# One block up to the output projection, with the sample attention merged into the gates stage

## The chip, the cores and the metric

The kernel runs on one core of a Trainium2 chip. A core has five engines with a queue of instructions each: TensorE (PE), VectorE (DVE), ScalarE (ACT), GpSimd (POOL) and SyncE (SP), which here only issues transfers, and 16 DMA engines. The engines run side by side and meet at semaphores. The metric is the device time of one execution in microseconds (us).

## The reference, cut to what matters

One layer of a hybrid decoder for 1024 prompt tokens and 64 sample tokens (8 sequences of 8), 1088 in all, width 1024, in float32:

```python
p = split(x @ w_in)                        # GLA, FoX, conv and three gates
o_gla  = gla(p) ; o_conv = B * conv3(C * h)
o_fox  = softmax(q k^T / 8 + decay, causal) v            # prompt: 8 heads, 1024 keys
o_fox_s = the same for the sample; per sequence 2 pages of 128 past keys,
          values and log-forget rows, gathered by page_table, and 8 new keys
br = stack([o_gla, o_fox, o_conv]) @ w_branch            # per branch 512 -> 1024
m  = sum_j sigmoid(x @ w_gate_j) * br_j                  # merge of three branches
x  = LN(alpha * x + m @ w_out)
x  = LN(alpha * x + moe(x))                              # router, 16 experts, top 2
```

## The kernel before

Every large float32 product is three products of parts: an operand is split into a high part (a copy by ACT, the *head*) and a low part (a subtraction by DVE, the *tail*), and PE computes hi x hi, lo x hi, hi x lo. Weights come by SP's DMAs into `slab_raw`, and their parts lie in `slab_hi` and `slab_lo`. PE writes into eight banks (`ps`).

The program is a sequence of stages: `stage_front` (input projection of GLA and convolution and all they compute), `stage_fox` (prompt attention, its q, k, v projections included), `stage_fox_sample`, `stage_gates`, `stage_out` (output projection, norm and routing) and `stage_experts`. Each of the first five opens an `nc.Block` of its own. At the end of a block every engine takes part in a barrier, and GpSimd's part comes after its stores have landed. Nothing of the next stage is issued on any engine before.

`stage_fox`: 12 weight blocks of 128 columns. The first two are loaded during the front (`load_fox_block`), their heads and tails are the first work of ACT and DVE behind the barrier. PE computes values (two halves), then keys and queries, and for each of 32 units Q (a pair of heads by a block of 128 queries) scores, transposes of probabilities and value products. Between these stand pieces of the next projections. On DVE `normalise(Q)` multiplies by the reciprocal of the sums, and a transpose on PE waits for it.

`stage_fox_sample` (L1463 to 1749): for 16 pages PE makes four transposes of keys (L1564) and four score products with 16 columns (L1575); ACT and DVE copy the transposed keys in turns; then, for four pairs of heads, row scores, maximum, exponent, transposes and 33 value products each (L1621, L1624). SP issues a page of keys and its log-forget row in pairs, with one load of the page number from SBUF for each pair; GpSimd issues the pages of values. Six key pages fit at a time (`RK`). At the end stands the head and tail of the first gate weights. No other products stand between.

`stage_gates` (L1790): for each of three branches j, in four steps of 2 column chunks, PE computes for each chunk three units (384, 384 and 320 tokens) of gate products over k = 0 to 7, then three units of branch products over k = 0 to 3 with the stored outputs `oT_hi`, `oT_lo` read back into `oh`, `ol`. Gate units use banks 0 to 3, branch units 4 to 7. ACT writes the sigmoid into `sg`, DVE multiplies by the branch product and adds to `m`, which GpSimd has set to zero (`m_clear`), after `gt_first`, a write of one element that lets the others start. Branches 0 and 1 run in a hardware loop over j. The 12 weight steps are loaded and split one or two steps ahead. SP reads `oh` and `ol` of a branch once the branch before it is done (`m_done`).

`stage_out` begins behind the gates' barrier, with the tails of the first token tiles of `m` already issued (`out_m_tails`, L1787).

## Time and profile before

| | us |
|---|---|
| three runs | 1872.73, 1865.41, 1867.82 |
| median | 1867.82 |
| profiled execution, its own time | 1866.79 |
| its span | 1865.1 |

Busy shares of the span: PE 89%, DVE 45%, ACT 35%, GpSimd 13%. By stage, from PE's side (the granted clock is 1.00 at 2.4 GHz and 0.50 at 1.2):

| stretch | us | PE busy | granted clock |
|---|---|---|---|
| front, 0 to 419.4 | 419.4 | 397.6 | 0.98 |
| block end, to 434.1 | 14.7 | 0.0 | 0.62 |
| prompt attention, to 767.2 | 333.1 | 308.0 | 0.96 |
| block end, to 781.4 | 14.2 | 0.0 | 0.52 |
| sample attention and block end, to 874.7 | 93.3 | 84.3 | 0.50 |
| gates, branch 0, to 1027.4 | 152.7 | 147.0 | 0.97 |
| gates, branches 1 and 2, to 1317.3 | 289.9 | 285.8 | 1.00 |
| block end, to 1322.3 | 5.0 | 0.0 | 0.83 |
| output, routing, experts | 542.8 | 438.8 | 0.89 |

How to read it: PE's busy time says how much of a stretch PE worked, but not at which clock; a stretch in which it is nearly always busy at 0.50 can hold as much lost time as one in which it stands. A row of the timeline has the start, the duration, the engine, the line and the operands, then in brackets the idle time of the engine ahead of it and who released it.

### The profile page before, as it was taken

The page shows a single profiled execution, that of the slowest core. Times are in us where ns is not written, and L with a number is a line of the kernel's source. Part 1 is how long each engine was busy: PE and PEld are TensorE (multiplying, and loading weights), DVE is VectorE, ACT ScalarE, POOL GpSimd, SP SyncE. Part 2 cuts the span into 40 slices and gives each one's busy share as a digit, 9 for nine tenths or more (in the row PEclk, how much of TensorE's full clock was granted, in tenths as well). Part 3 has the DMA queues.
Part 4 walks back from the last instruction along what each step waited for, and adds up shares of the span by engine and source line. Part 5 has one row for each costly group of instructions (what it writes and reads, how often), then busy time and mean ns, then how long its engine had stood idle before and what let it go on. Part 6 is the DMA issues. An engine that isn't in the chain of part 4 may idle for free. (4 is left out here: it accounts for less than half of the span.)

```text
span 1865.1 us, 25855 instructions
## 1 busy us (share of the span) xinstructions
PE 1661.6 (89%) x9847; PEld 1522.3 (82%) x9847; DVE 834.4 (45%) x1341; ACT 650.1 (35%) x1076; POOL 246.0 (13%) x320
## 2 busy tenths in 40 slices
PE   7999999996999998698999999999899299999950
PEld 6988898896988887597999999999788278888840
DVE  3433453441033343120222322222363689999947
ACT  4422322112154453211111211111211188888852
POOL 1000120021011111213000000000000123333114
PEclk9999999998999998655999999999999599999985
DMA  5111131123302110242311321320231678988538
GB/s 167 37 35 47 59 118 35 44 89 102 95 26 73 35 45 19 70 158 82 121 35 35 130 68 34 130 68 1 103 113 57 209 237 277 325 308 308 193 124 254
DMA packets 155300, 208.33 MB, mean 112 GB/s; under 512 B 14835, under 2 KB 121347, under 8 KB 155176
## 3 DMA queue, kind: packets, MB, share of 16 engines
q1 hardware_dynamic: 132472, 130.86, 22.7%
q0 software_dynamic: 22704, 75.79, 12.0%
q8 instruction: 81, 1.33, 0.3%
q14 instruction: 43, 0.35, 0.1%
HBM read 161.78 MB, written 44.84 MB: 111 GB/s over the span
## 5 line engine op out<-in xcount | busy, mean ns | idle before, releaser
L1852 PE MATMUL ps<-xh,slab_hi 128*128 128x384 f32 (+1 forms) x576 | 189.2, 328 | 8.3 <-POOL gt_first L1813 5.9
L1852 PE MATMUL ps<-xl,slab_hi 128*128 128x384 f32 (+1 forms) x576 | 188.8, 328 | 0.0
L1852 PE MATMUL ps<-xh,slab_lo 128*128 128x384 f32 (+1 forms) x576 | 188.8, 328 | 0.0
L375 PE MATMUL ps<-xh,slab_hi 128*128 128x384 f32 (+1 forms) x504 | 173.2, 344 | 1.2 <-DVE xl L730 1.2
L1895 DVE TENSOR_TENSOR gt_sg<-ps,gt_sg 128x384 f32<-128x384 f32 (+1 forms) x72 | 38.6, 536 | 293.9 <-PE ps L1852 293.9
L375 PE MATMUL ps<-xl,slab_hi 128*128 128x384 f32 (+1 forms) x504 | 166.5, 330 | 0.0
L375 PE MATMUL ps<-xh,slab_lo 128*128 128x384 f32 (+1 forms) x504 | 166.4, 330 | 0.0
L1867 ACT ACTIVATE gt_sg<-ps 128x384 f32<-128x384 f32 (+1 forms) x72 | 34.0, 474 | 298.6 <-PE ps L1852 298.5
L1852 PEld LDWEIGHTS ps<-xh,slab_hi 128*128 128x128 f32 x576 | 109.0, 189 | 9.0 <-issue 7.5
L1852 PEld LDWEIGHTS ps<-xh,slab_lo 128*128 128x128 f32 x576 | 109.0, 189 | 0.0
L1852 PEld LDWEIGHTS ps<-xl,slab_hi 128*128 128x128 f32 x576 | 109.0, 189 | 0.0
L375 PEld LDWEIGHTS ps<-xh,slab_hi 128*128 128x128 f32 x504 | 96.1, 191 | 15.3 <-issue 12.0
L1852 PE MATMUL ps<-gt_oh,slab_hi 128*128 128x384 f32 (+1 forms) x288 | 94.9, 330 | 7.4 <-DMA gt_ol<-oT_lo 7.4
L2517 PE MATMUL ps<-mo_hi_gu,mo_xh 128*128 128x512 f32 x256 | 100.3, 392 | 0.0
L2517 PE MATMUL ps<-mo_hi_gu,mo_xl 128*128 128x512 f32 x256 | 100.0, 391 | 0.0
L375 PEld LDWEIGHTS ps<-xl,slab_hi 128*128 128x128 f32 x504 | 96.2, 191 | 0.0
L375 PEld LDWEIGHTS ps<-xh,slab_lo 128*128 128x128 f32 x504 | 96.2, 191 | 0.0
L1852 PE MATMUL ps<-gt_ol,slab_hi 128*128 128x384 f32 (+1 forms) x288 | 94.7, 329 | 0.0
L1852 PE MATMUL ps<-gt_oh,slab_lo 128*128 128x384 f32 (+1 forms) x288 | 94.7, 329 | 0.0
L2459 POOL DMA_INDIRECT mo_xg<-x_dram,mo_slot_idx x32 | 70.0, 2188 | 167.4 <-PE ps L2505 142.1
L1331 ACT ACTIVATE fx_PT<-ps 128x512 f32<-128x512 f32 (+3 forms) x96 | 43.8, 494 | 110.0 <-PE ps L1209 110.0
L1158 PE MATMUL ps<-xh,slab_hi 128*128 128x384 f32 (+1 forms) x192 | 69.4, 362 | 11.4 <-DVE fx_kl L1390 6.8
(463 smaller groups left out, 3945.9 us busy)
## 6 DMA issues: line engine op xcount, KB each, us to landing
slab_raw<-in_w_in SPq DMA_DIRECT2D x60, 512.0 KB, 4.3
mo_raw_g<-in_w_e_gate SPq DMA_DIRECT2D x16, 1024.0 KB, 6.1
mo_raw_u<-in_w_e_up SPq DMA_DIRECT2D x16, 1024.0 KB, 9.0
mo_raw_d<-in_w_e_down SPq DMA_DIRECT2D x16, 1024.0 KB, 5.1
y_dram<-mo_y POOLq DMA_DIRECT2D x32, 512.0 KB, 4.2
gt_oh<-oT_hi SPq DMA_DIRECT2D x3, 2176.0 KB, 8.1
gt_ol<-oT_lo SPq DMA_DIRECT2D x3, 2176.0 KB, 13.1
slab_raw<-in_w_branch SPq DMA_DIRECT2D x24, 256.0 KB, 6.1
```

The source lines that it names most:

```text
L375: mm = eng.matmul(out, w[:, b, k, :], x[:, k, t0:t0 + tn], start=(k == 0 and j == 0), stop=(k == KC - 1 and j == 2), skip_group_check=True)
L1158: mm = eng.matmul(out, w[:, b % RH, k, :], x[:, k, t0:t0 + tn], start=(k == 0 and j == 0), stop=(k == KC - 1 and j == 2), skip_group_check ...
L1331: eng.activation(PT[:, h, 4 * c:4 * c + nt, :].rearrange("p t n -> p (t n)"), sh.ps[:, 5 + C % 2, 0:128 * nt], ACT.Copy).then_inc(pt_out, 1)
L1852: last = eng.matmul(out, w[:, s % 2, c, wk, :], x[:, k, t0:t0 + tn], start=(k == 0 and i == 0), stop=(k == ks[-1] and i == 2))
L1867: eng.activation(sg[:, v % 4, 0:tn], sh.ps[:, v % 4, 0:tn], ACT.Sigmoid).then_inc(sg_ready, 1)
L1895: eng.tensor_tensor(sg[:, v % 4, 0:tn], sh.ps[:, 4 + v % 4, 0:tn], sg[:, v % 4, 0:tn], ALU.mult).then_inc(mul_done, 1)
L2459: eng.indirect_dma_start(out=xg[:, i % RX, :], out_offset=None, in_=sh.x1_dram[:, :], in_offset=bass.IndirectOffsetOnAxis(ap=mo.slot_idx[: ...
L2517: eng.matmul(sh.ps[:, 2 + r, :], x[:, r, k, :], hi_gu[:, r, k].rearrange("p m n -> p (m n)"), start=(k == 0 and j == 0), stop=False)
```

## The change

All stages up to the output projection now stand in one block. What a stage needs of an earlier one is waited for by single semaphores: `sh.front`, `sh.fox` and `sh.gates` hold pairs of a semaphore and its last value. PE's first product of the prompt attention waits for the front's banks, its state and its last transposed output; stores and transfers are waited for by the engine that reuses their memory.

Four things move with it. (1) The first two weight blocks of the prompt attention get head and tail within the front's queues. (2) The first gate weights are loaded once the last keys are placed and split at Q = 24 of the prompt attention, on DVE ahead of `normalise(24)`. (3) `stage_fox_sample` is gone. Its work stands in `stage_gates`, in which the 24 gate units of branch 0 come first, cut into 96 pieces of six products (two k each) that stand between the page loop, the row scores, the transposes and the value products; the latter come in four parts of four sequence pages with a piece between parts. These gate units use banks 4 and 7, and their sigmoid goes straight to `sh.m`, so that branch 0's products are multiplied in place: the clearing of `m` and `gt_first` are gone. Key pages, probabilities and masks lie in parts of `m`, `sg` and the weights' raw buffer that are free at the time, with four key pages at a time. The branch products of j = 0 follow, then j = 1 and 2 as before, without a loop, with banks chosen by `gate_bank` and `branch_bank`. (4) The gate weights of branch 0 are loaded in two kinds of steps: 0 to 3 hold only the gate part, 4 to 7 only the branch part; 8 to 15 both. The output projection's loads wait for the gates' last branch product, and its products for `m_done`.

```diff
# stage_front: blocks 0 and 1 of the prompt attention in ACT's and DVE's queues
             def head(n):
+                if n >= RH:
+                    eng.wait_ge(unit_mm, ends[n - RH] + 1)
+                if n in (n_block, n_block + 1):
+                    head_fox(sh, eng, n - n_block)
                 if n >= n_block:
                     return
...
             def tail(n):
+                if n in (n_block, n_block + 1):
+                    tail_fox(sh, eng, n - n_block)
# stage_fox, PE
+            for bank in range(2):
+                eng.wait_ge(*sh.front.unit_free[bank])
+            eng.wait_ge(*sh.front.bank2)
+            eng.wait_ge(*sh.front.s0_new)
+            eng.wait_ge(*sh.front.o_out)
# stage_fox, ACT and DVE
+                if Q == 24:
+                    eng.wait_ge(unit_mm, kq_unit(3, 1, 2) + 1)
+                    head_gates(sh, eng, 0)
...
+                if Q == 24:
+                    tail_gates(sh, eng, 0)
                 eng.wait_ge(exp_done, 2 * Q + 2)
                 normalise(Q)
# stage_gates, SP
+            eng.wait_ge(*sh.fox.v_st)
+            eng.wait_ge(*sh.fox.pv_done)
+            for i in range(3):
+                load_page(i)
+            load_gates(sh, eng, 1)
+            for i in range(3, RK):
+                load_page(i)
+            for i in range(2):
+                eng.wait_ge(*sh.fox.o_st[i])
+            for i in range(NP):
+                load_logf(i)
+            eng.dma_start(cneg[:, :], sh.c_dram[1, :, SEQ:TOK]).then_inc(c_in, 16)
+            for i in range(RK, NP):
+                load_page(i)
+            load_gates(sh, eng, 2)
+            load_gates(sh, eng, 3)
+            eng.wait_ge(pv_mm, 4)
+            load_branch(0)
+            load_gates(sh, eng, 4)
             eng.wait_ge(oT_lo, 2)
...
+            for j in (1, 2):
+                eng.wait_ge(m_done, UJ * j)
+                load_branch(j)
+                for s in range(1, 5 if j == 1 else 4):
+                    load_gates(sh, eng, 4 * j + 4 + s)
# stage_gates, PE
+            gate_pieces(0, FIRST)
             for i in range(NP + 1):
                 if i < NP:
                     transpose_keys(i)
                 if i >= 1:
                     past_scores(i - 1)
+                gate_piece(FIRST + i)
             eng.wait_ge(pool_s, POOL_DONE)
             decay()
+            gate_pieces(25, 27)
             eng.wait_ge(c_in, 16)
             row_scores(0)
+            gate_pieces(27, 29)
             row_scores(1)
+            gate_pieces(29, 31)
             transpose_probs(0)
...
+            weigh_between(3, 55)
+            gate_pieces(58, 96)
+            for s in range(4):
+                eng.wait_ge(split, 4 + s + 1)
+                for c in range(2):
+                    branch(0, s, c)
# stage_gates, ACT
+            first_gate(0)
+            head_gates(sh, eng, 1)
+            first_gate(1)
+            for i in range(0, NP, 2):
+                place_keys(i)
+                if i % 4 == 2:
+                    first_gate(2 + i // 4)
+            exponent(0)
+            first_gate(6)
+            exponent(1)
+            place_probs(0)
+            first_gate(7)
+            exponent(2)
+            head_gates(sh, eng, 2)
+            first_gate(8)
+            place_probs(1)
+            first_gate(9)
+            exponent(3)
+            first_gate(10)
...
# stage_out, SP
+            eng.wait_ge(*sh.gates.br_mm)
             for k in range(TB, KC):
                 eng.dma_start(w_raw[:, k - TB, :], sh.w_out[0, 128 * k:128 * k + 128, :]).then_inc(w_in[k - TB], 16)
```

On PE, between the front and the prompt attention, before (L418 is the front's last transpose, L1144 the first value projection; `fr_` names belong to the front):

```order
L418 MATMUL ps<-ident,fr_st 18x128 [waits fr_b2_free,fr_st_ready]
L160 UNCONDITIONAL_BRANCH
L1129 UNCONDITIONAL_BRANCH [waits barrier_Pool_Activation_PE_DVE_SP_release]
L1144 MATMUL ps<-slab_hi,xh 128x256 [waits fx_w_tail]
L1144 MATMUL ps<-slab_hi,xl 128x256
```

And after the change (L426 and L1176 are the same two steps):

```order
L426 MATMUL ps<-ident,fr_st 18x128 [waits fr_b2_free,fr_st_ready]
L1161 UNCONDITIONAL_BRANCH
L1176 MATMUL ps<-slab_hi,xh 128x256 [waits fr_s0_new,fr_o_out,fr_b2_free,fox_tail,fr_unit_free1,fr_unit_free0]
L1176 MATMUL ps<-slab_hi,xl 128x256
L1176 MATMUL ps<-slab_lo,xh 128x256
```

The wait for the barrier and for the tail behind it has become one product that waits for semaphores of the front and for `fox_tail`, whose instructions stand earlier.

On PE, the page loop of the sample attention, before (L1564 transposes of a key page, L1575 its scores):

```order
L1564 MATMUL ps<-ident,fs_kp 128x128 [waits fs_k_out,fs_k_in2]
L1564 MATMUL ps<-ident,fs_kp 128x128 x3
L1575 MATMUL ps<-fs_qbd,fs_KT 128x16 [waits fs_k_out]
L1575 MATMUL ps<-fs_qbd,fs_KT 128x16 x3
L1564 MATMUL ps<-ident,fs_kp 128x128 [waits fs_k_out,fs_k_in3]
```

And after the change (L1743 transposes, L1754 scores, L1729 a gate piece; `m` and `gt_sg` hold the key pages and their transposes):

```order
L1743 MATMUL ps<-ident,m 128x128 [waits gt_k_out,gt_k_in0]
L1743 MATMUL ps<-ident,m 128x128 x3
L1754 MATMUL ps<-slab_raw,gt_sg 128x16 [waits gt_k_out]
L1754 MATMUL ps<-slab_raw,gt_sg 128x16 x3
L1729 MATMUL ps<-xh,slab_hi 128x384 [waits gt_sg_ready]
L1729 MATMUL ps<-xl,slab_hi 128x384
L1729 MATMUL ps<-xh,slab_lo 128x384
```

A gate piece of six wide products, three of them shown, now stands between the narrow ones of two pages, and here waits for the sigmoid of an earlier unit.

On SP, the pages (L1542) and log-forget rows (L1544) of the sample, before (L1503 loads the page number):

```order
L1503 TENSOR_LOAD pages
L1503 ISA x2
L1542 ISA
L1542 DMA fs_kp<-in_cache_fox_k 128x512
L1544 ISA
L1544 DMA fs_lf<-in_cache_fox_logf 128x8
```

And after the change, from behind page 2 on (L1664 a key page, L1669 a log-forget row, L1518 gate weights, L1619 the load of a page number):

```order
L1518 DMA slab_raw<-in_w_in 128x8x128 [waits g_split]
L1518 DMA slab_raw<-in_w_in 128x8x128
L1619 TENSOR_LOAD pages
L1619 ISA x2
L1664 ISA
L1664 DMA m<-in_cache_fox_k 128x512
L1619 TENSOR_LOAD pages [waits fx_o_st1,fx_o_st0]
L1619 ISA x2
L1669 ISA
L1669 DMA gt_lf<-in_cache_fox_logf 128x8
```

The pair is taken apart: a row now has its own load of the page number, and sixteen rows stand between page 3 and page 4, which then waits for the keys' buffer:

```order
L1669 ISA
L1669 DMA gt_lf<-in_cache_fox_logf 128x8
L1687 DMA gt_cneg<-c_dram 8x64
L1619 TENSOR_LOAD pages [waits gt_k_tr]
L1619 ISA x2
L1664 ISA
L1664 DMA m<-in_cache_fox_k 128x512
```

Ahead of page 4 there are now the last of these rows and the transfer of the sample's running decay.

On DVE at Q = 24, after the change (L1475 the low part of an output, L1466 and L1470 `normalise`, L1541 the tail of the gate weights; before, L1423 followed L1432 at once):

```order
L1460 ISA fx_P,fx_low<-ps,fx_cb 128x256 [waits fx_s_mm,fx_p_tr]
L1460 ISA fx_low 128x1
L1475 TENSOR_TENSOR fx_ol<-ps,fx_oh 128x128 [waits fx_oT_hi]
L1541 TENSOR_TENSOR slab_lo<-slab_raw,slab_hi 128x2x1024 [waits g_head]
L1466 RECIPROCAL fx_rinv<-fx_rsum 128x2 [waits fx_exp_done]
L1470 TENSOR_TENSOR fx_o_tm<-ps,fx_rinv 128x128 [waits fx_oT_tr,fx_pv_done,fx_dve]
```

The tail of the gate weights stands between them and waits for its head on ACT.

## Rows read from the trace of the kernel before

**Rows 1.** Windows: stretch, length; busy (count) PE, PEld, DVE, ACT, POOL; PEclk, DMA share, GB/s

```profile
434.10:439.90 5.80, 5.80 (x27) 5.80 (x28) 0.00 (x0) 0.00 (x0) 0.20 (x1) 0.50 1.02 324
440.00:488.00 48.00, 48.00 (x405) 48.00 (x404) 4.81 (x4) 10.21 (x21) 0.00 (x0) 1.00 0.25 68
600.00:707.00 107.00, 100.15 (x776) 93.04 (x775) 39.83 (x133) 49.95 (x130) 17.18 (x31) 1.00 0.12 36
710.00:755.00 45.00, 36.63 (x230) 30.45 (x228) 16.32 (x60) 16.98 (x48) 6.41 (x12) 0.77 0.06 19
781.40:869.00 87.60, 84.31 (x386) 80.44 (x386) 13.07 (x33) 11.50 (x23) 16.34 (x22) 0.50 0.35 112
767.20:1027.40 260.20, 231.36 (x1251) 226.97 (x1251) 55.42 (x103) 37.52 (x60) 28.71 (x37) 0.78 0.29 88
1027.40:1173.00 145.60, 142.88 (x864) 142.36 (x864) 39.14 (x52) 23.61 (x30) 0.00 (x0) 1.00 0.25 75
893.70:896.70 3.00, 2.96 (x10) 2.96 (x11) 0.00 (x0) 0.00 (x0) 0.00 (x0) 0.54 1.18 294
```

**Rows 2.** Timeline, start, duration, engine, line, [idle <-releaser]: end of the front

```profile
420.23 0.25 ACT L605 ACTIVATE fr_st_tm<-ps 18x128 f32<-18x128 f32 x1
...
430.49 2.00 ACT L1263 ACTIVATE slab_hi<-slab_raw 128x1024 fp32r<-128x1024 f32 x2 [10.01 <-PEq L160]
...
434.09 0.58 PE L1144 MATMUL ps<-slab_hi,xh 128*128 128x256 f32 x1 [14.69 <-DVE slab_lo L1383]
```

**Rows 3.** Timeline: start of the output projection, DVE and PE

```profile
1318.38 3.49 DVE L1787 TENSOR_TENSOR xl<-m,xh 128x1024 fp32r<-128x1024 f32 x3
...
1322.34 0.77 PE L2005 MATMUL ps<-slab_hi,xh 128*128 128x512 f32 x1 [5.00 <-PEq L1794]
...
1323.33 0.63 PE L2005 MATMUL ps<-slab_lo,xh 128*128 128x512 f32 x1
...
1323.76 0.63 PE L2005 MATMUL ps<-slab_hi,xh 128*128 128x512 f32 x1
```

**Rows 4.** Timeline, PE in the gates stage: first branch product, second branch's first

```profile
893.74 0.55 PE L1852 MATMUL ps<-gt_oh,slab_hi 128*128 128x384 f32 x1 [4.40 <-DMA gt_ol<-oT_lo]
...
1027.38 0.43 PE L1852 MATMUL ps<-xh,slab_hi 128*128 128x384 f32 x1 [1.26 <-DVE m L1898]
```

**Rows 5.** Groups by form: xcount, busy us, mean ns, idle: heads and tails of weights

```profile
L1263 ACT ACTIVATE slab_hi<-slab_raw 128x1024 fp32r<-128x1024 f32 x12 | 12.4, 1049 | 21.8 <-DMA slab_raw<-in_w_in 11.8 <-PEq L160 10.0
...
L1769 ACT ACTIVATE slab_hi<-slab_raw 128x3072 fp32r<-128x3072 f32 x12 | 33.3, 2773 | 67.9 <-PE ps L1852 55.7 <-DMA slab_raw<-in_w_branch 12.2
...
L1383 DVE TENSOR_TENSOR slab_lo<-slab_raw,slab_hi 128x1024 fp32r<-128x1024 f32 x12 | 14.6, 1232 | 58.0 <-ACT slab_hi L1263 58.0
...
L1775 DVE TENSOR_TENSOR slab_lo<-slab_raw,slab_hi 128x3072 fp32r<-128x3072 f32 x11 | 36.9, 3359 | 31.7 <-ACT slab_hi L1769 31.7
```

**Rows 6.** Timeline: prompt attention near its 24th query block

```profile
713.63 0.20 ACT L1320 ACTIVATION_READ_ACCUMULATOR fx_P<-fx_P,fx_low 128x1 f32 x1
...
714.30 0.29 DVE L1427 TENSOR_TENSOR fx_o_tm<-ps,fx_rinv 128x128 f32<-128x128 f32 x1 [0.73 <-DVE fx_rinv L1423]
```

**Rows 7.** Timeline, weight loads (PEld) of value products: prompt at 568, sample at 832

```profile
568.12 3.24 PEld L1224 LDWEIGHTS ps<-fx_v,fx_PT 128*128 128x128 f32 x28
...
832.68 6.90 PEld L1624 LDWEIGHTS ps<-fs_PT,fs_vp 128*128 128x128 f32 x32 [0.22 <-issue]
```

**Rows 8.** Timeline: a table load on ACT; SP's queue (SPq) issuing pages and log-forget rows

```profile
884.96 1.28 ACT L1867 ACT_TABLE_LOAD   x1
...
778.63 0.38 SPq L1542 DMA_DIRECT2D fs_kp<-in_cache_fox_k  x1
...
783.56 0.33 SPq L1544 DMA_DIRECT2D fs_lf<-in_cache_fox_logf  x1
...
784.65 0.33 SPq L1542 DMA_DIRECT2D fs_kp<-in_cache_fox_k  x1
```

**Rows 9.** The page's DMA issues: xcount, KB each, median us to landing

```profile
gt_ol<-oT_lo SPq DMA_DIRECT2D x3, 2176.0 KB, 13.1
```

588 lines of the change are left out of this document (334 added, 254 removed).

## The prediction

> **What bounds the kernel now.** I read the busy shares of the page first, then windows by stage, then the instructions around each stage's end. TensorE (PE) works in 89% of the span, and in the gates stage it is the bound: one pass over a branch takes 145.6 us, 142.9 of it PE work, at a granted clock of 1.00 [rows 1]. So time can only be won where PE stands still or runs at 1.2 instead of 2.4 GHz. The windows show three such places, and each is the end of a block. After the front stage PE stands for 14.7 us [rows 2], then works 5.8 us at 0.50 [rows 1]. From 767.2 (the last product of the prompt attention) to 781.4 it stands again; then comes the whole sample attention, 87.6 us at 0.50 although PE is 96% busy, and after it the first branch pass [rows 1]. Before the output projection there are 5.0 us of standing [rows 3].
>
> **The change, part by part.**
>
> *Front to prompt attention.* PE's last product there is a small transpose whose result ScalarE (ACT) copies until 420.48 [rows 2]. The rest of the gap is no work of PE's: GpSimd waits until the stage's stores have landed, the barrier opens, and only then, from 430.49, are the first two weight blocks split (two heads, two tails), until PE starts at 434.09. After the change two blocks are split within the front stage and PE waits for that copy alone, so it starts at about 420.6: 434.1 - 420.6 = 13.5 us. The 27 products at half clock take 5.8 us [rows 1]; at the pace of the next window (405 in 48.0 us, 0.119 each) they take 3.2, and after a gap of 1.2 us I expect no half clock, since the gap of 1.26 us at 1027.38 [rows 4] was followed by a pass at 1.00. That is 2.6 more: **-16.1 us**. The first two splits (1.05 on ACT, 1.23 on VectorE (DVE) each [rows 5]) now stand in the front's queues; both engines have room there, with shares of 35% and 45% over the span: **+0.5** (0 to 1.5). The stores go on landing behind the value products. The key placement, the first user of their buffers, comes some 50 us later.
>
> *The first gate weights, split at Q = 24.* ACT gets 2048 columns, between 1.05 for 1024 and 2.77 for 3072 [rows 5]: 1.9 us. It begins after the exponent whose sum is read until 713.83 and ends at 715.75; the next copy on ACT was due at about 715.5 and loses 0.3 us. DVE waits for it, takes 2.3 us (between 1.23 and 3.36 [rows 5]), and stands ahead of the normalisation that stood at 714.30 [rows 6]: it now comes at about 718.4, and PE's transpose of its result waits for it. All behind it moves by the same: **+4** (2 to 6), as this tail of the stage runs on such chains (PE busy 36.6 of 45 us, clock 0.77 [rows 1]).
>
> *Sample attention within the gates.* Before, the stretch from 767.2 to 1027.4, where the first branch is done, takes 260.2 us [rows 1]. What PE has to do there afterwards is the same work: one pass of gate and branch products, 142.9 us, and the 386 narrow products of the sample [rows 1] (128 scores of past keys, 64 transposes of pages, 128 value products, 66 others). At half clock 32 of them cost 6.9 us, 0.215 each; at full clock the nearest rows are the value products of the prompt, 3.24 us for 28, 0.116 each [rows 7]. With gate pieces between them I take the full clock: 386 x 0.116 = 44.8 us. Bounds for it are 44.8 and 83.0.
>
> Stalls in it, in order. (1) The head of gate weights 1 stands in ACT's queue ahead of the first key copy. A gate piece is six products, 142.9 x 2/3 / 96 = 0.99 us on average, 1.04 in the wide groups. PE reaches the first page after 8 wide pieces, at 775.5; the weights (issued at about 770.9, 4 us to land for 512 KB and here 1 MB behind three pages) are copied by 777.0, the sigmoid and the key copy follow, and PE waits **1.0**. (2) SyncE (SP) issued a page and its log-forget row in pairs; from a row's issue to the next page's it is 1.09 us (783.56 to 784.65), which holds the load of the page number [rows 8]. Now the sixteen rows come by themselves, each with its own load: 1.09 x 16 = 17.4 us, and they stand ahead of page 4. SP begins with the last value product, at about 766.4; three pages, two weight loads of 0.6, page 3 and the rows put page 4 at about 791, landed at 793.9 (2.8 us as for page 0, issued at 778.63 [rows 8] and used at 781.40). PE does a page and a piece in 12 x 0.116 + 0.99 = 2.4 us and, after four transposes of pages, three of scores and four pieces, is there at 784.7: it waits **9.2** (5 to 11). Later pages come every 1.1 us and are hidden. (3) After such a wait the clock falls: after the 4.4 us for a DMA before 893.74 [rows 4] the next 3 us ran at 0.54 [rows 1]; I take the 2.4 us that the same costs at the output projection, **2.3**. (4) ACT gets nine table loads, as Exp and Sigmoid now alternate, 1.28 us each [rows 8]. From the first scores to the first value products ACT has 0.8 (maximum) + 2.0 + 1.8 + 2.0 + 0.4 = 7.0 us of it, PE 10.7 us of other work (eight pieces and two score groups): hidden, 0. (5) The wait ahead of the second branch is one DVE operation shorter, 0.6 for 1.26 [rows 4].
>
> By the Trainium skill ("ScalarE: Activation LUTs", What ACT_TABLE_LOAD costs) a switch costs a drain besides, 2.66 us together. In this trace the load at 884.96 took 1.28 us and its row has no idle time ahead of it [rows 8], so no drain shows. By the page's figure ACT's chain would be about 11 us against PE's 10.7, and the sum some 1 to 3 us longer.
>
> Sum: 142.9 + 44.8 + 1.0 + 9.2 + 2.3 + 0.6 = 200.8, against 260.2: **-59.4 us**. Hidden within the pieces: the gate weights' later splits, the memset of m (no longer there), and the load of the first branch, which cost PE 4.4 us before.
>
> *Second and third branch.* Weight load 9 (and 13) now comes behind the loads of oh and ol and stands, as a head, ahead of ACT's first sigmoid. Before, oh and ol (4.4 MB) landed 13.1 us after their issue with a part of a weight load beside them [rows 9]; with all of 1.5 MB more in the same stretch I take 15 to 18 us. Then head and tail (2.8 + 3.4), sigmoid and two DVE operations (1.6): 22.8 to 25.8 us. PE needs the first freed bank after a block's gates (11.9, two thirds of 142.9/8), the wait for ol that is there already (1.5), its branch products (5.9) and one more unit (4.2): 23.5. An even race, **+2** for both (0 to 8).
>
> *Gates to output.* The last tail that PE needs, the first of three of 1.16 us that follow 1318.38 [rows 3], is done at 1319.54, so PE starts at 1319.6 and not at 1322.34: **-2.7**. After 5.0 us of standing 12 products ran at 0.43 us each (1323.33 to 1323.76 [rows 3]) and the next at 0.23: 2.4 us; with 2.3 us of standing half of that may stay: **-1.2**.
>
> Sum: -16.1 + 0.5 + 4 - 59.4 + 2 - 2.7 - 1.2 = **-72.9**. The profiled execution took 1866.8 us (span 1865.1 and 1.7 around it), so 1793.9; the median of the three runs is 1867.8, 1 us more. I forecast 1794.
>
> **The rivals.**
>
> *Clock low in the page loop.* In the sample stage PE was 96% busy and stayed at 0.50 [rows 1], so narrow products do not bring the clock back. After the wait for page 4 it may stay low until the last page. Price: 192 products x 0.099 = 19.0, and 17 pieces x 0.81 (six products at 0.30, as the 10 in the 3 us behind 893.7 [rows 1], against 0.165) = 13.8, less the 2.3 in the sum: +31, **1825**. For it: 1.4 us of narrow products stand between two pieces. Against: the prompt attention up to 707 mixes runs of 3.2 us of narrow products with such pieces and holds 1.00 [rows 1]. Chance 0.18.
>
> *Clock low throughout (the slower side).* From the hitch at Q = 24 to piece 58 PE runs at 1.2 GHz. Price: 386 x 0.099 = 38.2, 50 pieces x 0.81 = 40.5, and the attention's tail, 36.6 us at 0.77, at 0.50 for +20, less 2.3: +96, **1890**. It decides once it eats more than the 73 us. The tail of that stage, where no pieces are mixed in, fell to 0.77 [rows 1]. Chance 0.05.
>
> *ACT decides the merged stage.* First gate sigmoids wait behind exponents, heads and nine table loads, and PE, with two gate banks, waits for them. If all loads (11.5 us) show: **1806**. Chance 0.12.
>
> *No wait for page 4,* because SP is faster than its rows suggest: without 9.2 and 2.3, **1782**. Chance 0.15.
>
> *The change doesn't merge anything:* if pieces only fill PE's waits but each narrow product keeps its 0.215, at full clock for the rest: +38, 1832. Since cost and clock go together in the trace, chance 0.04.
>
> **How the numbers follow.** The forecast, 1784 to 1806, has 0.46; the other cases 0.18, 0.05, 0.12, 0.15, 0.04 as above. The range takes in all but the slow end and the far ends of the small terms: 1774 to 1834. A measurement here can tell 0.5% (9 us) from no change. Faster by more than that holds in all cases but the second: 0.93, with 0.04 for within and 0.03 for slower, as partial forms of that rival end near zero.
>
> **What would show it.** PE's gap after the front under 2 us, at 1.00; a DVE normalisation some 4 us late at Q = 24; one PE wait of 5 to 11 us for a page DMA, the fifth, and none at later pages; narrow products at 0.116 each; 200 us from the end of attention to the second branch; nine table loads with no PE wait on ACT behind them. I am wrong if the granted clock in the merged stage stays near 0.5, or if PE waits for sigmoids.

## The result, and the profile after

The changed kernel takes 1806.56 us (median of 4 runs, 1802.15 to 1807.92), against 1867.47 us before (4 runs). The ratio is 0.967, with a 95% interval of 0.964 to 0.970. The profiled execution took 1802.15 us, the shortest of the four, with a span of 1800.5 us: 64.6 us less than the span before.

The same five marks on PE in both traces give the stages: the first product of the prompt attention, its end (before the change the end of its last product, after it the first gate product, which follows at once), the first product of the second branch, the last of the third, and the first of the output projection.

| stretch | before | after | difference | forecast |
|---|---|---|---|---|
| to the prompt attention | 434.1 | 420.75 | -13.3 | -13.0 |
| prompt attention, to its last product | 333.1 | 330.4 | -2.7 | +1.4 |
| from there to the second branch | 260.2 | 205.2 | -55.0 | -59.4 |
| second and third branch | 290.0 | 296.2 | +6.2 | +2 |
| stop ahead of the output projection | 5.0 | 2.4 | -2.6 | -2.7 |
| output projection to the end | 542.8 | 545.6 | +2.8 | -1.2 |
| sum | 1865.1 | 1800.5 | -64.6 | -72.9 |

The windows after (columns as in [rows 1]) answer to them: the beginning of the attention, its tail, the two parts of the merged stage, the second and the third branch, and the first 3 us of the output projection.

```profile
420.70:426.50 5.80, 5.75 (x48) 5.78 (x49) 2.58 (x3) 2.13 (x3) 2.33 (x5) 1.00 0.63 178
693.70:751.10 57.40, 45.53 (x317) 38.50 (x317) 20.80 (x70) 24.78 (x61) 8.57 (x16) 0.82 0.06 19
751.10:908.10 157.00, 147.57 (x963) 144.32 (x964) 24.22 (x55) 38.83 (x65) 14.54 (x34) 0.93 0.37 112
908.10:956.30 48.20, 47.55 (x290) 47.29 (x288) 19.44 (x28) 6.29 (x5) 0.00 (x0) 1.00 0.20 55
956.30:1104.70 148.40, 144.45 (x864) 143.64 (x864) 38.87 (x52) 22.14 (x28) 0.00 (x0) 0.99 0.25 73
1104.70:1252.50 147.80, 142.87 (x864) 142.06 (x864) 37.92 (x51) 24.65 (x31) 0.00 (x0) 1.00 0.24 74
1254.90:1257.90 3.00, 2.96 (x7) 2.41 (x8) 2.81 (x3) 1.51 (x2) 0.00 (x0) 0.50 1.01 389
```

The start of the attention, which had 5.80 us at 0.50, is at 1.00. The sample's 386 products no longer have a stretch of their own at 0.50: they lie in the 157 us from 751.1, at 0.93. And these are the places where PE now stands (timeline, with the idle time and its releaser in brackets):

```profile
420.75 0.36 PE L1176 MATMUL ps<-slab_hi,xh 128*128 128x256 f32 x1 [1.28 <-DVE fr_y L800]
```

```profile
764.67 1.04 PE L1754 MATMUL ps<-slab_raw,gt_sg 128*128 128x16 f32 x8 [3.21 <-ACT gt_sg L1903]
...
781.22 1.11 PE L1743 MATMUL ps<-ident,m 128*128 128x128 f32 x4 [6.23 <-DMA m<-in_cache_fox_k]
```

```profile
956.35 0.41 PE L1826 MATMUL ps<-xh,slab_hi 128*128 128x384 f32 x1 [0.70 <-issue]
...
970.61 0.44 PE L1826 MATMUL ps<-gt_oh,slab_hi 128*128 128x384 f32 x1 [2.16 <-DMA gt_ol<-oT_lo]
...
983.17 0.44 PE L1826 MATMUL ps<-xh,slab_hi 128*128 128x384 f32 x1 [0.63 <-DVE m L2026]
```

```profile
1104.77 0.44 PE L1826 MATMUL ps<-xh,slab_hi 128*128 128x384 f32 x1 [1.18 <-DVE m L2026]
...
1119.58 0.44 PE L1826 MATMUL ps<-gt_oh,slab_hi 128*128 128x384 f32 x1 [2.70 <-DMA gt_ol<-oT_lo]
...
1132.09 0.44 PE L1826 MATMUL ps<-xh,slab_hi 128*128 128x384 f32 x1 [2.16 <-DVE m L2026]
```

```profile
1254.94 0.77 PE L2180 MATMUL ps<-slab_hi,xh 128*128 128x512 f32 x1 [2.41 <-DVE xl L1553]
```

The gap of 14.69 us [rows 2] is 1.28. Where 14.2 us of standing and the slow sample stood, there are two waits, 3.21 us for the first key copy and 6.23 us for page 4. The branches have more waits than before: a second one for DVE, and a longer one for ol than the 1.4 and 1.6 us of before.

### The profile page after: what moved, and what is told of

Same layout as the page of the kernel before. It is cut to its first block and busy times, and to the rows that moved or that the text cites. A ratio compares the mean times of both kernels' runs of the same rounds, so it can differ in the third digit from the quotient of the medians.

```text
span 1800.5 us, 25622 instructions
## 1 busy us (share of the span) xinstructions
PE 1620.9 (90%) x9847; PEld 1481.8 (82%) x9847; DVE 823.8 (46%) x1322; ACT 658.1 (37%) x1087; POOL 231.7 (13%) x317
## 3 DMA queue, kind: packets, MB, share of 16 engines
q8 instruction: 78, 1.28, 0.3%
## 5 line engine op out<-in xcount | busy, mean ns | idle before, releaser
L383 PE MATMUL ps<-xh,slab_hi 128*128 128x384 f32 (+1 forms) x504 | 173.4, 344 | 2.5 <-DVE xl L742 2.5
L383 PE MATMUL ps<-xh,slab_lo 128*128 128x384 f32 (+1 forms) x504 | 166.8, 331 | 0.0
L383 PE MATMUL ps<-xl,slab_hi 128*128 128x384 f32 (+1 forms) x504 | 166.6, 331 | 0.0
L1826 PE MATMUL ps<-xh,slab_hi 128*128 128x384 f32 (+1 forms) x384 | 125.5, 327 | 4.7 <-DVE m L2026 4.0
L1826 PE MATMUL ps<-xh,slab_lo 128*128 128x384 f32 (+1 forms) x384 | 125.1, 326 | 0.0
L1826 PE MATMUL ps<-xl,slab_hi 128*128 128x384 f32 (+1 forms) x384 | 125.0, 326 | 0.0
L383 PEld LDWEIGHTS ps<-xh,slab_hi 128*128 128x128 f32 x504 | 96.5, 192 | 16.6 <-issue 12.0
L2023 DVE TENSOR_TENSOR gt_sg<-ps,gt_sg 128x384 f32<-128x384 f32 (+1 forms) x48 | 25.7, 535 | 162.3 <-PE ps L1826 162.3
L383 PEld LDWEIGHTS ps<-xl,slab_hi 128*128 128x128 f32 x504 | 96.5, 191 | 0.0
L383 PEld LDWEIGHTS ps<-xh,slab_lo 128*128 128x128 f32 x504 | 96.3, 191 | 0.0
L1541 DVE TENSOR_TENSOR slab_lo<-slab_raw,slab_hi 128x3072 fp32r<-128x3072 f32 (+2 forms) x16 | 40.9, 2559 | 108.3 <-ACT slab_hi L1534 108.3
L1966 ACT ACTIVATE gt_sg<-ps 128x384 f32<-128x384 f32 (+1 forms) x48 | 22.3, 473 | 167.4 <-PE ps L1826 167.4
L1190 PE MATMUL ps<-xh,slab_hi 128*128 128x384 f32 (+1 forms) x192 | 69.4, 362 | 11.4 <-DVE fx_kl L1433 6.8
L1534 ACT ACTIVATE slab_hi<-slab_raw 128x3072 fp32r<-128x3072 f32 (+2 forms) x16 | 34.1, 2129 | 122.2 <-PE ps L1826 59.4
## 6 DMA issues: line engine op xcount, KB each, us to landing
gt_ol<-oT_lo SPq DMA_DIRECT2D x3, 2176.0 KB, 13.8
```

Of the source, the lines that this page charges most:

```text
L383: mm = eng.matmul(out, w[:, b, k, :], x[:, k, t0:t0 + tn], start=(k == 0 and j == 0), stop=(k == KC - 1 and j == 2), skip_group_check=True)
L1190: mm = eng.matmul(out, w[:, b % RH, k, :], x[:, k, t0:t0 + tn], start=(k == 0 and j == 0), stop=(k == KC - 1 and j == 2), skip_group_check ...
L1534: eng.activation(hi[:, n % 2, :, ks], raw[:, :, ks], ACT.Copy).then_inc(sh.g_head, 1)
L1541: eng.tensor_tensor(lo[:, n % 2, :, ks], raw[:, :, ks], f32(hi[:, n % 2, :, ks]), ALU.subtract).then_inc(sh.g_split, 1)
L1826: last = eng.matmul(out, w[:, s % 2, c, wk, :], x[:, k, t0:t0 + tn], start=(k == 0 and i == 0), stop=(k == ks[-1] and i == 2))
```

## The experiments

Twelve kernels, each an edit of the changed kernel. Since the changes that matter here are of a few us, the length of the stages in each profile is given beside the medians. "Attention" is from its first product to its last transpose, "gates" from there to the last branch product, "rest" from the first product of the output projection to the end.

| kernel | median us | profiled us | attention from | attention | gates | rest |
|---|---|---|---|---|---|---|
| before | 1867.5 | 1866.8 | 434.1 | 332.8 | 549.8 | 542.8 |
| changed | 1806.6 | 1802.2 | 420.8 | 330.2 | 500.9 | 545.6 |
| no_mix | 1847.4 | 1852.4 | 423.2 | 338.1 | 542.2 | 544.3 |
| whole | 1809.9 | 1811.0 | 421.1 | 328.9 | 511.5 | 544.9 |
| w1_early | 1805.6 | 1802.8 | 423.8 | 328.4 | 499.6 | 546.4 |
| pages_first | 1796.3 | 1792.0 | 424.0 | 330.3 | 488.6 | 544.4 |
| w1_pages | 1788.8 | 1784.7 | 419.0 | 328.9 | 487.5 | 544.6 |
| early9 | 1799.5 | 1798.4 | 420.3 | 330.2 | 498.8 | 544.4 |
| ol_alone | 1797.1 | 1796.0 | 420.1 | 328.8 | 495.7 | 546.7 |
| q24_behind | 1807.4 | 1804.1 | 421.7 | 330.5 | 500.9 | 546.4 |
| clear1 | 1803.4 | 1808.5 | 423.6 | 334.2 | 501.9 | 544.2 |
| out_own | 1808.5 | 1815.6 | 421.3 | 334.1 | 508.7 | 544.2 |
| front_wait | 1810.4 | 1810.8 | 425.3 | 333.3 | 502.3 | 545.1 |
| best | 1782.6 | 1782.6 | 418.5 | 334.1 | 480.7 | 544.7 |

The table also shows how far a stage moves by itself. Eight kernels (changed, no_mix, whole, pages_first, early9, ol_alone, clear1, out_own) have the same code up to the end of the attention. It starts at 420 to 424 in them and takes 328.8 to 338.1 us, 331.9 on average.

### no_mix: the narrow products in one stretch

```diff
-                gate_piece(FIRST + i)
...
-            gate_pieces(25, 27)
...
-            gate_pieces(58, 96)
+            gate_pieces(FIRST, 96)
```

All pieces from the ninth on stand behind the last value products; ACT's and DVE's queues are put in the order that follows from it.

> The changed kernel without the interleaving: the first eight gate pieces, then all 386 narrow products of the sample attention in one stretch, then the other 88 pieces. Everything else (one block, banks, buffers, weights, order of the transfers) stays. Theory A (the pieces between them keep the clock up): the narrow stretch runs at 0.50 and costs 0.215 us per product as before the change, 38 us more in PE work, and waits of the chains of maximum, exponent and transposes show, 5 to 15 us: about 1845 to 1855 us. Theory B (the single block and the absence of long stops keep the clock up, the pieces do nothing): narrow products at 0.12 us, clock near 1.00, and only the waits show: about 1810 to 1820 us.

Measured: 1847.42 us, ratio to before 0.989 (0.987 to 0.991). The windows of a stretch with narrow products alone, and of the gate pieces behind the last:

```profile
790.00:820.00 30.00, 28.94 (x142) 28.94 (x142) 4.15 (x6) 4.87 (x7) 1.61 (x3) 0.50 0.57 176
...
880.00:900.00 20.00, 20.00 (x124) 20.00 (x123) 2.29 (x1) 4.15 (x6) 0.00 (x0) 1.00 0.03 3
```

PE is busy throughout and the clock stays at 0.50 until wide products come, as in the sample stage before [rows 1]. So theory A holds: 41 us of the 61 that the change gained hang on the gate pieces between the narrow products (PE's waits in the page loop, 9.9 and 4.0 us for 6.2 and 3.2, are 4.5 of these), and all the rest of the change, the single block with its shorter stops above all, gives some 20. In this kernel, as before the change, the clock went down at a wait at or near the start of the narrow stretch; how long such a stretch would hold 1.00 without one was not tried.

### whole: the value products in one run

```diff
                 for part in range(4):
                     weigh_values(p, part)
-                    if part < 3:
-                        gate_piece(n + part)
+                gate_pieces(n, n + 3)
```

> The changed kernel with the 33 value products of each pair of heads in one run, and the three gate pieces that stood between their parts behind them. The order is otherwise the same. Theory A (a run of narrow products of about 4 us between pieces does not bring the clock down, as in the prompt attention, where 28 to 32 of them stand together at 1.00): the clock stays 1.00 in the stretch of the value products, and the stage from the first gate piece to the second branch keeps its length within 2 us; about 1806 us. Theory B (the four parts are what keeps the clock up there): the clock falls to about 0.5 within or behind each run of value products, 4 runs of some 4 to 8 us at half clock, 8 to 16 us longer.

Measured: 1809.87 us, ratio 0.970 (0.968 to 0.971), so not told apart from the changed kernel by time. In the profile, two of the windows in the stretch of the value products are below 1.00:

```profile
830.10:840.10 10.00, 10.00 (x64) 9.62 (x64) 3.49 (x5) 5.08 (x6) 0.00 (x0) 0.83 0.30 77
...
870.10:880.10 10.00, 10.00 (x64) 10.00 (x64) 1.26 (x8) 1.92 (x10) 0.00 (x0) 0.83 0.59 215
```

In the changed kernel every window of 10 us from 791 to 951 is at 1.00. 17% of 10 us, twice, is 3.4 us: less than the 8 of theory B, more than the nothing of theory A. PE had not stood still there (10.00 us busy in both windows), so the narrow products alone brought the clock down, behind two of the four runs of 33 and for a short time. The other 7 us by which "gates" is longer lie in the page loop and the two later branches, which this edit doesn't touch (out_own, with the same code there as the changed kernel, is 7.8 us longer too). In this profile the four parts are worth some 3 us.

### w1_pages, w1_early, pages_first: the two waits of the page loop

```diff
# weights early (w1_early, w1_pages)
+            load_gates(sh, eng, 1)
             eng.wait_ge(*sh.fox.v_st)
             eng.wait_ge(*sh.fox.pv_done)
...
# pages first (pages_first, w1_pages)
-            for i in range(NP):
-                load_logf(i)
...
             for i in range(RK, NP):
                 load_page(i)
+                load_logf(i - RK)
```

> The changed kernel with two waits of PE in the page loop taken away: gate weights 1 are issued ahead of the pages (behind the first split, before the attention's end), and the sixteen log-forget rows are issued behind the pages that used to stand behind them, one row with each page from page 4 on. After the change PE waited 3.2 us for the first key copy, behind the head of these weights, and 6.2 us for page 4, and ran 13.4 us of work at 1.2 GHz around them. Theory A (the clock fell because PE stood still there): both waits go, the granted clock stays 1.00 from 751 on, the stage is 3.2 + 6.2 + 6.7 = 16 us shorter, about 1790 us. Theory B (narrow products bring the clock down by themselves, whatever the waits): both waits go, the clock still falls in the page loop, and the gain is 9 us or less. Theory C: pages come too slowly for PE once each takes a row with it (1.1 us for a pair against 2.4 us of PE work for a page and a piece); a wait returns at a later page or at the last rows.

> The changed kernel with gate weights 1 issued ahead of the pages alone; the log-forget rows still stand ahead of page 4. With both edits PE waited nowhere in the page loop, the clock stayed at 1.00 and the kernel took 1788.8 us. Theory A (the transfers of page 4 are set by SyncE's queue, whatever PE does): the 3.2 us wait for the key copy goes, PE comes to page 4 earlier and waits there for longer, 9 to 13 us, and the clock is low for some us behind it: gain 1 to 6 us, about 1803 us. Theory B (the waits are worth their length each): 3 to 4 us of wait and the half clock ahead of page 4 go, about 1799 us, with 6 us of wait left at page 4.

> The changed kernel with the log-forget rows behind the pages alone; gate weights 1 still stand behind page 2. Theory A (one standstill is enough to bring the clock down, and pages are there when PE comes): the wait of 6.2 us at page 4 goes, that of 3.2 us stays, the clock is at 0.50 for a few us behind it and back by 775: gain 6.2 and about 3 us of half clock, about 1797 us. Theory B (once down, the clock stays down while narrow products and pieces alternate): 0.50 to the end of the page loop, and no gain or a loss.

First, what SyncE did in the changed kernel: the sixteen rows in one piece, and the pages behind them, five in this row.

```profile
759.02 16.71 SPq L1669 DMA_DIRECT2D gt_lf<-in_cache_fox_logf  x16
...
777.11 6.31 SPq L1664 DMA_DIRECT2D m<-in_cache_fox_k  x5
```

16.71 us for the rows, and page 4 issued at 777.11. The waits of PE that were left in w1_early (line and releaser, total us, times, longest):

```profile
PE ps L1741 <- DMA m<-in_cache_fox_k: 12.3, 1, 12.3
```

The one in pages_first, and two windows there, in and behind this wait:

```profile
PE ps L1755 <- ACT gt_sg L1904: 2.8, 1, 2.8
```

```profile
764.00:768.00 4.00, 1.15 (x11) 0.94 (x9) 1.38 (x1) 2.78 (x3) 1.76 (x6) 1.00 0.37 125
768.00:772.00 4.00, 4.00 (x34) 3.98 (x34) 1.51 (x2) 0.60 (x1) 1.83 (x4) 1.00 0.57 157
```

And the second of these windows in w1_pages, which had no such wait:

```profile
768.00:772.00 4.00, 4.00 (x32) 3.93 (x31) 0.06 (x1) 0.60 (x1) 1.63 (x4) 1.00 1.00 338
```

- **w1_early**, 1805.6 us (ratio 0.969, 0.966 to 0.971): the wait for the key copy is gone, and the one for page 4 has grown from 6.23 to 12.3 us. A wait removed ahead of a later one that a queue sets is not a gain. Theory A.
- **pages_first**, 1796.3 us (0.964, 0.962 to 0.967): no page is waited for, 2.8 us are left for the key copy, and the clock did not fall at all behind them. The gain of 10 us is near the 9 of theory A, but theory A had expected a half clock behind the first wait that did not come.
- **w1_pages**, 1788.8 us (0.958, 0.957 to 0.960): no wait at all in the loop, the clock 1.00 throughout, 17.7 us less. Theory A.

The gains don't add: 1 and 10 us singly, 17.7 together.

### early9 and ol_alone: the transfers at a branch's start

```diff
+                load_gates(sh, eng, 4 * j + 5)
                 eng.wait_ge(m_done, UJ * j)        # ol_alone: br_mm
                 load_branch(j)
+                eng.wait_ge(o_in, 32 * j + 32)     # ol_alone only
-                for s in range(1, 5 if j == 1 else 4):
+                for s in range(2, 5 if j == 1 else 4):
```

> The changed kernel with the first weight step of the second and of the third branch issued ahead of the wait for the branch before, not behind the loads of oh and ol. After the change PE waited 2.2 and 2.7 us for ol and 0.6 and 2.2 us for DVE in the next block, and 3 us ran at about half clock in the second branch, where before it was 1.6 and 1.4 us for ol and nothing else: 6.3 us more. Theory A (the place of that weight load makes both the later ol and the late sigmoids): the waits for DVE go, those for ol fall to 1.6 us or less, the two branches are 5 to 7 us shorter, about 1801 us. Theory B (ol is bound by its own 4.4 MB at about 300 GB/s, 14.6 us, whatever else is issued): the wait for ol stays over 2 us, only the waits for DVE go, 3 us shorter at most.

> The kernel with the first weight step of the second and third branch issued ahead, and in addition oh and ol issued as soon as PE's last branch product is done (1.2 us earlier, not behind DVE's last addition) and the next weight steps only once ol has landed. With the first of these alone PE still waited 2.0 and 2.7 us for ol: 4.4 MB took 14.1 us from issue to use, with weights beside them from 7.6 us on. Theory A (the weights beside it make ol late): ol lands 3 to 4 us earlier and PE does not wait for it; no half clock behind it; the second and third branch take 145 and 144 us, 1800 us or less. Theory B (4.4 MB by themselves take 13 to 14 us on the DMA engines): PE's wait falls only by the 1.2 us of the earlier issue, to about 1 us each.

Measured: early9 1799.45 us (0.966, 0.963 to 0.969), ol_alone 1797.06 us (0.963, 0.962 to 0.964). The wait for ol in the second branch of early9 (in the third it is 2.73 us):

```profile
969.83 0.44 PE L1827 MATMUL ps<-gt_oh,slab_hi 128*128 128x384 f32 x1 [2.01 <-DMA gt_ol<-oT_lo]
```

And in ol_alone, where nothing else is loaded, the issue of ol and the product that waits for it:

```profile
953.42 0.51 SPq L1674 DMA_DIRECT2D gt_ol<-oT_lo  x1
```

```profile
967.91 0.44 PE L1828 MATMUL ps<-gt_oh,slab_hi 128*128 128x384 f32 x1 [2.13 <-DMA gt_ol<-oT_lo]
```

The additional wait for DVE is gone in both, as theory A had it. The waits for ol are not: in ol_alone it is used 14.5 us after its issue with nothing beside it, and in early9 13.8 us after it (956.05 to 969.83), with a weight step beside it from 963.28 on. In the changed kernel, with a weight step issued right behind it, it was 13.9 us (956.73 to 970.61). So theory B holds for ol: 4.4 MB in 14.5 us are 300 GB/s, and this transfer is bound by itself. What ol_alone gained at the third branch (1.39 us of wait instead of 2.70) is its earlier issue. The two branches together are 2.1 us shorter in early9 and 4.7 us in ol_alone than in the changed kernel; the medians moved by 7.1 and 9.5 us, and the six runs of early9 lie between 1794.7 and 1811.4, so what is above these lengths isn't shown to come from the edits.

### q24_behind: the split behind the normalisation

```diff
-                if Q == 24:
-                    tail_gates(sh, eng, 0)
                 eng.wait_ge(exp_done, 2 * Q + 2)
                 normalise(Q)
+                if Q == 24:
+                    tail_gates(sh, eng, 0)
```

> The changed kernel with the tail of gate weights 0 on DVE behind the normalisation of Q = 24 and not ahead of it; the head on ACT stays. After the change PE stood 2.3 us for this normalisation, and yet the rest of the attention had caught up with the course before the change by its end, with a granted clock of 1.00 where it had been 0.65 before. Theory A (the standstill costs its length, and the catching up is a chance of the clock): PE's wait of 2.3 us goes and the stage is 2 to 4 us shorter. Theory B (what PE loses there it does not need later, or the half clock comes at another place): the standstill goes or moves, and the length of the stage stays within 1 us of 330.4 us. By medians neither can be told from no change, so the stage's length and its windows in the profile decide.

Measured: 1807.41 us (0.970, 0.967 to 0.972), attention 330.5 against 330.2 us. In the changed kernel, the tail, the normalisation and PE's wait for it:

```profile
699.70 2.29 DVE L1541 TENSOR_TENSOR slab_lo<-slab_raw,slab_hi 128x2048 fp32r<-128x2048 f32 x1 [2.16 <-ACT slab_hi L1534]
...
702.10 0.29 DVE L1470 TENSOR_TENSOR fx_o_tm<-ps,fx_rinv 128x128 f32<-128x128 f32 x1
...
702.45 0.47 PE L1247 MATMUL ps<-ident,fx_o_tm 128*128 128x128 f32 x1 [2.27 <-DVE fx_o_tm L1470]
```

The wait of 2.27 us did go in q24_behind, and this one came instead, for DVE's next output:

```profile
PE ps L1256 <- DVE fx_ol L1475: 7.8, 6, 3.0
```

Its longest is 3.0 us, where before and after the change no such wait was over 1.5. So theory B: the 2.3 us of DVE have to be somewhere in this chain, and the place changes nothing that shows.

### front_wait: the front's stores waited for again

```diff
             eng.wait_ge(*sh.front.o_out)
+            for r in range(len(sh.front.o_st)):
+                eng.wait_ge(*sh.front.o_st[r])
+            eng.wait_ge(*sh.front.gla_st)
```

> The changed kernel with one wait put back: PE's first product of the prompt attention also waits until the front's stores (the transposed outputs and the state) have landed, as the block's end made it do before. No barrier, and the first two weight blocks stay split in the front's queues. Before the change the barrier opened at 430.49, 10 us behind PE's last product, and the splits took 3.6 us more. Theory A (the landing of the stores makes up those 10 us, and the clock falls over them): PE stands 8 to 11 us and then works for 3 to 6 us at half clock: 10 to 13 us slower, about 1818 us. Theory B (the barrier itself, and what the engines do at a block's end, make up most): PE stands under 5 us and the loss is under 5 us.

Measured: 1810.38 us (0.970, 0.969 to 0.972), 3.8 us above the changed kernel.

```profile
425.28 0.55 PE L1176 MATMUL ps<-slab_hi,xh 128*128 128x256 f32 x1 [4.89 <-DMA oT_lo<-slab_lo]
```

```profile
425.28:429.60 4.32, 4.32 (x20) 4.32 (x21) 0.00 (x0) 0.00 (x0) 2.02 (x6) 0.50 0.83 235
```

PE stands 4.89 us (1.28 in the changed kernel), and its first 4.32 us behind that are at 0.50. So these stores make up half of the 10 us until the barrier opened; theory B. The other half shows in the trace of before, at the block's end (L160), as one instruction of GpSimd's queue, the `DRAIN` behind its last work (view by source: count; shortest, median and longest in ns; first and last start):

```profile
L160 POOLq DRAIN  x1: 5454/5454/5454, 424.8 to 424.8; - x1
```

It starts once the stores have landed and ends at 430.2; the barrier opened right behind it.

### clear1 and out_own: the end of the output stage

```diff
# clear1: semaphores without gaps, one sem_clear and not four
-        sh.dma_sem = lambda name: ctx.enter_context(nc.semaphore(name))
+        spare_sems = [ctx.enter_context(nc.semaphore(f"dma_sem{i}")) for i in range(19)]
+        sh.dma_sem = lambda name: spare_sems.pop(0)
# out_own: the block is left behind stage_gates, and stage_out gets one of its own
+            with nc.Block() as sh.block:
+                stage_out(nc, sh)
```

> The changed kernel with its semaphores numbered without gaps, so that the clearing at the end of the big block is one instruction over 138 semaphores and not four (57, 29, 32 and 20). In the profile after the change the stage end behind the last DVE operation of the output stage (1390.07 us) lasts until 1394.81, 4.74 us; before it was 0.8 us, with two clears of 91 semaphores. Theory A (each clearing instruction costs a fixed time, about 2 us): the stretch falls to under 1 us and the time by 4 us or somewhat more. Theory B (the cost goes with the number of semaphores, which stays 138): stretch and time stay. Theory C (the end of the long block costs something else, such as fetching instructions): stretch and time stay, too. 4 us is 0.2%, so the stretch in the profile decides, not the median.

> The changed kernel with the output stage in a block of its own again, as before the change; all else stays in the one block, and the clearing at its end is still four instructions over 138 semaphores. With the semaphores numbered without gaps (one clearing instruction) the end of the stage still took 4.2 us from the last DVE operation to the first of the experts, against 4.7 after the change and 0.8 before. Theory B (the cost goes with the number of semaphores cleared, 138 against 91): it stays at 4 to 5 us, and the block end ahead of the output projection costs some 2.5 us more: slower by about 2.5 us. Theory C (it is the end of a long block that costs, not the clearing): the end of the short block takes 0.8 us again, and the long block's end now stands ahead of the output projection, where PE waits for DVE's tails for 2.4 us anyway: a standstill of 5 to 7 us there, and the sum within 2 us of the changed kernel.

Measured: clear1 1803.43 us (0.966, 0.964 to 0.968), out_own 1808.51 us (0.970, 0.968 to 0.973). The last DVE operation of the output stage and the first of the experts', in the changed kernel, in clear1 and in out_own:

```profile
1389.90 0.17 DVE L2277 TENSOR_TENSOR lg<-ps,wo_brb 128x16 f32<-128x16 f32 x1 [6.41 <-PE ps L2173]
...
1394.85 0.31 DVE L2428 TENSOR_REDUCE rt_a<-lg 128x9 f32<-128x144 f32 x1 [4.77 <-PEq L74]
```

```profile
1396.15 0.17 DVE L2277 TENSOR_TENSOR lg<-ps,wo_brb 128x16 f32<-128x16 f32 x1 [6.41 <-PE ps L2173]
...
1400.54 0.30 DVE L2428 TENSOR_REDUCE rt_a<-lg 128x9 f32<-128x144 f32 x1 [4.21 <-PEq L74]
```

```profile
1405.96 0.17 DVE L2277 TENSOR_TENSOR lg<-ps,wo_brb 128x16 f32<-128x16 f32 x1 [6.41 <-PE ps L2173]
...
1407.54 0.30 DVE L2428 TENSOR_REDUCE rt_a<-lg 128x9 f32<-128x144 f32 x1 [1.41 <-PEq L74]
```

4.78, 4.22 and 1.41 us of idle DVE, against 0.8 before. Three clearing instructions less are worth 0.5 us, so it is neither their number (theory A) nor the 138 semaphores (theory B): out_own clears the same in 1.4. What out_own takes away is that the output stage ends the long block, and the traces show which engine that end waits for. It is GpSimd, with the `DRAIN` of its queue behind its last stores. In the changed kernel, and in out_own at the end of the output stage:

```profile
L2986 POOLq DRAIN  x1: 6520/6520/6520, 1386.9 to 1386.9; - x1
```

```profile
L3006 POOLq DRAIN  x1: 777/777/777, 1403.0 to 1403.0; - x1
```

The first ends at 1393.43, 3.4 us behind DVE's last operation (1390.07), when every other engine has finished, and the barrier opens then. The second ends at 1403.76, before DVE is done, and costs nothing; before the change it took 0.79 us at this place. The long block of out_own has its own `DRAIN` of 5.79 us, but at 791.57, where GpSimd's work in this block was over; it is hidden behind 470 us of the others, and PE went on 0.5 us behind DVE's last tail (1269.23 to 1269.71). So the 4 us are 3.4 of GpSimd's `DRAIN` and some 0.5 of more clearing. Why it takes 5 to 7 us at the end of one block and 0.8 at the end of another isn't shown: nine transfers issued by GpSimd in the block went with 0.78, 66 (the front before) with 5.45, 82 (the prompt attention before) with 6.74, 173 (the long block) with 6.52, so it isn't their number alone.

### best: the edits that gained, together

The edits of w1_pages and ol_alone, and in `stage_gates`:

```diff
             for j in (1, 2):
-                eng.wait_ge(m_done, UJ * j)
+                eng.wait_ge(sg_ready, UJ * j)
...
                     for k in ks:
+                        if kind == "gate" and v == 0 and k == ks[-1]:
+                            eng.wait_ge(m_done, UJ * j)
```

> The edits that gained, together: gate weights 1 ahead of the pages, log-forget rows behind the pages, the first weight step of the second and third branch ahead of the wait, oh and ol issued right behind the last branch product with no weights beside them, and PE's wait for DVE's last addition moved from the first product of a branch to the last of its first unit. If the gains add: 17.7 us of the page loop, 5 to 6 us of the branches and 1.5 us of the moved wait, from 1806.6: about 1782 us. If the clock falls at another place once these stops are gone, 1788 us as without the branch edits.

Measured: 1782.63 us (1778.96 to 1787.88), ratio to before 0.955 (0.953 to 0.957): 24 us less than the changed kernel.

```profile
PE ps L1829 <- DMA gt_ol<-oT_lo: 5.3, 2, 2.8
PE ps L2183 <- DVE xl L1553: 2.4, 1, 2.4
```

```profile
752.60:952.00 199.40, 199.40 (x1321) 196.82 (x1322) 47.11 (x84) 48.83 (x73) 16.55 (x34) 1.00 0.39 124
```

In the 199.4 us from the first gate piece PE is busy all the time at 1.00. The waits for ol (5.3 us, two times) and the one ahead of the output projection are what is left up to there.

## Why the prediction was right, and where it was off

The median of 1806.6 lies in the range, the direction and the size were right, and it is 12.6 us above the forecast of 1794. The profiled execution, by which the sum was made, is 1802.2, 8.3 above it; the other 4.4 us are that between this execution and the median (by the prediction's own words the median lies 1 us above its profile, which would have made 1795). The median also lies on the price of a rival, 1806 for "ACT decides", and just outside the 1784 to 1806 of the forecast; that this rival isn't the cause is read from the waits, not from the number. And part of the nearness is luck: three terms were 4.4, 4.2 and 4.0 us too low, and the attention gave 4.1 back, with a clock in its tail that varies from one execution to the next. By step:

- **Front to prompt attention, -16.1 + 0.5: right.** PE starts at 420.75 for 420.6, and the clock stays at 1.00 over the gap of 1.28 us. The two splits in the front can't be seen: the attention starts at 418.5 to 424 in the twelve kernels without the added wait.
- **Split at Q = 24, +4: the mechanism was right, the sum wasn't.** DVE's tail took 2.29 us and PE stood 2.27 us for the normalisation behind it. Yet the attention was 330.4 us long where 334.5 would have followed. The step that failed is "All behind it moves by the same". This tail of the attention runs at a clock that differs from one execution to the next (the windows below, 306 to 321 us behind the stage's first product; the last two kernels have the same code up to there), and the stage's length varies by 9 us with the same code; against that the average of the eight (331.9) is 1.7 us more than 332.8 less the 2.6 us of clock. So the term may be of that size, and q24_behind could not give it back. Before, after, and in no_mix:

```profile
740.00:755.00 15.00, 13.59 (x73) 11.01 (x73) 5.27 (x17) 4.37 (x11) 1.07 (x2) 0.65 0.03 10
```

```profile
727.00:742.00 15.00, 12.28 (x103) 10.34 (x102) 6.75 (x22) 8.11 (x18) 2.15 (x4) 1.00 0.06 20
```

```profile
729.40:744.40 15.00, 13.10 (x74) 11.51 (x73) 3.98 (x15) 6.19 (x16) 2.14 (x4) 0.68 0.06 19
```

- **Merged stage, -59.4: measured -55.0.** The main term held. PE is busy for 147.57 + 47.55 = 195.1 us, and in windows of 10 us from 761.1 the missing clock makes 6.79 x 0.23 + 3.89 x 0.50 + 9.88 x 0.30 = 6.5 us of it:

```profile
761.10:771.10 10.00, 6.79 (x39) 6.53 (x38) 2.89 (x2) 3.37 (x4) 4.45 (x10) 0.77 0.40 106
771.10:781.10 10.00, 3.89 (x17) 3.49 (x15) 0.69 (x1) 0.44 (x1) 4.76 (x9) 0.50 0.84 238
781.10:791.10 10.00, 9.88 (x54) 9.76 (x55) 0.69 (x1) 1.19 (x2) 1.08 (x2) 0.70 0.71 246
```

  That leaves 188.6 for 187.7. If the wide work took its 142.9, a narrow product took 0.118 us for the 0.116 of the sum. Eight of the value products together took 1.03 us, but that isn't 0.129 for each more: with the 3.24 us for 28 before [rows 7] both fit 0.11 for each and 0.15 once for a run.

```profile
834.96 1.03 PEld L1804 LDWEIGHTS ps<-gt_sg,gt_vp 128*128 128x128 f32 x8
```

  The waits: (1) 3.2 us and not 1.0, since the weights needed 6.3 us from their second issue at 755.48 to ACT's head at 761.75, where I had taken 4; (2) 6.2 and not 9.2: page 4 was issued 26.0 us behind the first gate piece (23.8 in the sum) and took 4.1 us to its use (2.8), but PE came to it 23.9 us behind that piece and not 17.5, through (1) and the half clock; (3) the clock cost 6.5 and not 2.3, because it was already down ahead of page 4 when PE stopped again; (4) ACT's table loads: 0, as said; (5) 0.7 for 0.6. So the mis-sized terms are (1) and (3), 2.2 and 4.2 us, and (2) gave 3.0 back; with 0.9 of the products and 0.1 of (5) these are the 4.4.
- **ACT's table loads.** They come as expected, and nothing of PE's waits for them. Two of them stand around the second exponent, with the sigmoid between:

```profile
819.54 1.28 ACT L1896 ACT_TABLE_LOAD   x1
820.84 0.49 ACT L1896 ACTIVATE m<-ps 128x384 f32<-128x384 f32 x1
821.35 1.28 ACT L1909 ACT_TABLE_LOAD   x1
822.64 0.53 ACT L1909 ACTIVATE m<-ps,gt_nm 128x320 f32<-128x320 f32 x1
```

  1.28 us each and no idle time beside them, and between 791 and 908 PE is never idle. So the figure of 2.66 us for a switch (the Trainium skill, "ScalarE: Activation LUTs", What ACT_TABLE_LOAD costs) does not show in this trace either, and its drain cost nothing here.
- **Second and third branch, +2: measured +6.2.** "An even race" was lost both times. ol is late by 2.16 and 2.70 us (1.6 and 1.4 before), DVE by 0.63 and 2.16, and PE is busy for 144.45 us in the second branch where it had been 142.88, because the clock fell behind the wait. The failed step is the landing time: I left ol where it was before and let only the weights be late. ol was used 13.9 and 14.4 us behind its issue, where it had been 13.2 and 13.1; as it took 14.5 and 14.3 with nothing beside it (ol_alone), the weights aren't what made it later, and what did stays open.
- **Ahead of the output projection, -2.7 and -1.2: right.** PE stood 2.41 us, and the half clock lasted for 7 products and not 12, 5 x 0.2 = 1.0 us.
- **The end of the output stage: not in the sum.** 4 us more between DVE's last operation there and the experts' first (the output stage gave 0.6 back and the experts 0.5). Nothing in the diff moved this place, except that it is now the end of the long block, for which GpSimd's `DRAIN` takes 6.52 us and not 0.79; I priced no block end that the change keeps.

Of the rivals, "no wait for page 4" was wrong, and so was "clock low in the page loop" as put (from page 4 to the last page): the clock was back by 788. But a fifth of it was true, 6.5 of 33 us (its 31 and the 2.3 of the sum), and no_mix shows the mechanism behind it at its full size. "ACT decides" had its one trace in the 3.2 us, through the head of the weights and not through table loads.
